# Large products of a hybrid encoder layer as plain fp32 matmuls, with the weights loaded straight into a ring of four tiles

## The reference

```python
proj = rms_norm(h, mix_norm) @ w_in                      # 1024 x 2048
att  = mla_group(proj[..., :352], ...)                   # 8 heads of latent attention, chunk-causal
rw   = rwkv7_group(token_shift(proj[..., 352:], mu), ...)  # 8 heads of a linear recurrence
h = h + concatenate([att, rw]) @ w_out                   # 1024 x 1024
q = rms_norm(h, ca_norm) @ wq; k, v = rms_norm(mem, mem_norm) @ wkv   # 256 memory tokens
h = h + softmax(q k^T / 16) v @ wo                       # 4 heads of 256
h = h + square(relu(rms_norm(h, mlp_norm) @ w_up)) @ w_down   # 4096 hidden features
out = rms_norm(h, final_norm)
```

## Time and profile before

| what | value |
|---|---|
| time, median of 3 runs | 2378.82 us (2354.41 to 2385.33) |
| span of the profiled execution | 2361.8 us, first to last instruction |
| TensorE busy in it | 2097.7 us, 89% |
| VectorE, ScalarE, GpSimd busy | 854.9, 410.0, 477.2 us |
| mean granted TensorE clock | 0.900 of full speed |

### The profile page before, as it was taken

One profiled execution on the slowest core, in us unless ns is written; L12 is line 12 of the kernel. 1 busy time (PEld: TensorE's weight loads), 2 busy tenths in 40 slices (PEclk: granted clock), 3 DMA queues, 4 the chain that ended last, 5 costly groups with the idle time before them and its releaser, 6 DMA issues.

```text
span 2361.8 us, 28991 instructions
## 1 busy us (share of the span) xinstructions
PE 2097.7 (89%) x10464; PEld 1634.2 (69%) x10464; DVE 854.9 (36%) x1424; ACT 410.0 (17%) x762; POOL 477.2 (20%) x280
## 2 busy tenths in 40 slices
PE   5999779887988898889498798797999999999996
PEld 4887358546755664666388785586888888888885
DVE  5223463345345433643633503425311211211333
ACT  3001311221122122211311302202100100100210
POOL 2321010001001000100120130121433333333431
PEclk9997779857987796779699999898999999999998
DMA  3110120002000200010312210010111111111111
GB/s 133 53 44 13 45 61 2 9 1 61 2 10 7 54 1 10 21 41 1 125 39 85 89 53 1 18 44 27 46 52 44 53 44 53 44 51 47 44 53 71
DMA packets 74499, 97.86 MB, mean 41 GB/s; under 512 B 28720, under 2 KB 54832, under 8 KB 74160
## 3 DMA queue, kind: packets, MB, share of 16 engines
q1 hardware_dynamic: 74416, 96.76, 12.2%
HBM read 85.19 MB, written 11.55 MB: 41 GB/s over the span
## 4 chain that ended last, share of the span: by engine, by line
PE 74%; DVE 12%; issue 9%; ACT 2%; DMA 1%; POOL 1%; DVEq 0%; SPq 0%; ACTq 0%; POOLq 0%
PE PS L563 47%; PE PS L684 3%; PE PS L661 2%; PE PS L1046 1%; PE PS L675 1%; DVE tmp L1378 1%; PE PS L983 1%; PE PS L641 1%; PE PS L706 1%; PE PS L643 1%; PE PS L711 1%; PE PS L664 1%; PE PS L837 1%; PE PS L822 1%; PE PS L647 1%
## 5 line engine op out<-in xcount | busy, mean ns | idle before, releaser
L563 PE MATMUL PS<-xn,wsp 128*128 128x512 f32 x3456 | 795.8, 392 | 16.2 <-DVE xn L1371 13.0
L563 PEld LDWEIGHTS PS<-xn,wsp 128*128 128x128 f32 x3456 | 653.7, 189 | 157.3 <-issue 11.5
L563 PE MATMUL PS<-hid,wsp 128*128 128x512 f32 x1536 | 348.8, 389 | 0.0
L563 PEld LDWEIGHTS PS<-hid,wsp 128*128 128x128 f32 x1536 | 288.4, 188 | 59.8
L479 POOL CAST wsp<-wraw 128x1024 fp32r<-128x1024 f32 x104 | 110.5, 1062 | 918.5 <-PE PS L563 767.9
L481 POOL TENSOR_TENSOR wsp<-wraw,wsp 128x1024 fp32r<-128x1024 f32 x104 | 283.2, 2723 | 8.3
L1341 ACT ACTIVATE tmp<-PS 128x1024 f32<-128x1024 f32 x32 | 32.9, 1028 | 494.2 <-PE PS L563 494.2
L1859 DVE TENSOR_TENSOR tmp<-tmp 128x1024 f32<-128x1024 f32 x32 | 39.2, 1225 | 211.7 <-ACT tmp L1341 211.7
L1874 DVE TENSOR_TENSOR H<-PS,H 128x1024 f32 x24 | 29.4, 1225 | 218.6 <-PE PS L563 218.6
L661 PE MATMUL PS<-H 128*128 128x512 f32 (+2 forms) x192 | 101.8, 649 | 0.8 <-DVE H L1519 0.6
L684 PE MATMUL PS<-sa,H 128*128 x576 | 89.6, 312 | 4.8 <-DVE H L1533 4.8
(11 more groups left out here) (269 smaller groups left out, 2564.1 us busy)
## 6 DMA issues: line engine op xcount, KB each, us to landing
wraw<-in_weights_dram SPq DMA_DIRECT2D x120, 512.0 KB, 3.2
H<-in_x_dram SPq DMA_DIRECT2D x16, 512.0 KB, 7.3
H<-x_dram SPq DMA_DIRECT2D x32, 128.0 KB, 2.5
H<-xt_dram SPq DMA_DIRECT2D x32, 128.0 KB, 2.7
out_dram<-proj SPq DMA_DIRECT2D x8, 512.0 KB, 3.0
a_dram<-sc_w SPq DMA_DIRECT2D x12, 256.0 KB, 2.3
sc_s<-in_head_weights_dram SPq DMA_DIRECT2D x4, 320.0 KB, 3.0
x_dram<-sa SPq DMA_DIRECT2D x1, 1032.0 KB, 4.0
```

Of the source, the lines that this page charges most:

```text
L563: last = nc.tensor.matmul(PS[:, 2 * k + half, :], wsp[:, k, kt, a, :], src[:, kt, b, HALF * half:HALF * half + HALF], start=(kt == 0 and ( ...
```

## The change

The three passes become one plain fp32 matmul for each half, so the heads and rests go everywhere: the weights', the inputs', the memory tokens', the cross attention output's and the hidden tiles'. Weights go from DRAM into a ring of four tiles (`RING` = 4), and TensorE reads them there. SyncE refills a place of the ring when TensorE has finished the unit that was in it. The normed inputs are scaled directly into `xn`; the output product reads `mixed`. The memory values are made with the tokens as the stationary operand, so that they come out turned, in two products of 128 columns for each input tile. ScalarE's relu frees the accumulators. The reload of `x` no longer waits for rests. Places in memory are laid out anew. The core of the diff:

```diff
+        xn = sa[:, 0:8192].rearrange("p (k t) -> p k t", k=KT)
+        hid = proj[:, 0:KT, :]
+        ring = sc_s[:, :].rearrange("p (b k n) -> p b k n", b=RING, k=KT)
...
+        def done(u):
+            return u + RING + 1
+        def freed(u):
+            return u + 3
...
-                with sp.Fori(0, n // 2) as i:
-                    for k in range(2):
-                        if U_MK + 2 <= u0 <= U_Q + 1:
-                            sp.wait_ge(mem_split, 2 * i + (u0 - U_MK - 1 + k))
-                        else:
-                            sp.wait_ge(w_split, 2 * i + (by_pool(u0) + k + 1))
-                        sp.dma_start(wraw[:, k, :], wall[bass.ds(2 * i + (u0 + k), 1)].rearrange(
-                            "a p n -> (a p) n")).then_inc(raw_loaded[k], 16)
+                with sp.Fori(0, n // RING) as i:
+                    for b in range(RING):
+                        sp.wait_ge(acc_ready, RING * i + done(u0 + b - RING))
+                        sp.dma_start(ring[:, b], wall[bass.ds(RING * i + (u0 + b), 1)].rearrange(
+                            "a p (k n) -> (a p) k n", k=KT)).then_inc(w_loaded[b], 16)
...
-            weights(U_OUT, 2)
+            weights(U_OUT, RING)
             for kt in range(KT):
-                sp.wait_ge(xn_ready, KT + kt + 1)
                 sp.dma_start(H[:, kt, :], x_t[kt]).then_inc(x_loaded[kt], 16)
...
+            def unit(u, turn, b, src, ready):
+                k = b % 2
+                pe.wait_ge(w_loaded[b], 16 * (turn + 1))
                 pe.wait_ge(acc_free, u + 1)
                 for kt in range(KT):
                     ready(kt)
-                    for a, b in ((0, 0), (0, 1), (1, 0)):
-                        for half in range(2):
-                            last = nc.tensor.matmul(
-                                PS[:, 2 * k + half, :], wsp[:, k, kt, a, :],
-                                src[:, kt, b, HALF * half:HALF * half + HALF],
-                                start=(kt == 0 and (a, b) == (0, 0)), stop=(kt == KT - 1 and a == 1))
+                    for half in range(2):
+                        last = nc.tensor.matmul(PS[:, 2 * k + half, :], ring[:, b, kt, :],
+                                                src(kt)[:, HALF * half:HALF * half + HALF],
+                                                start=(kt == 0), stop=(kt == KT - 1))
...
+                    for t in range(2):
+                        for kt in range(KT):
+                            last = nc.tensor.matmul(PS[:, 2 * (b % 2), win(t)], memn[:, kt, win(t)], ring[:, b, kt, :],
+                                                    start=(kt == 0), stop=(kt == KT - 1))
...
-            def scale_and_split(n, pas, gain, between=lambda kt: None):
...
+            def scale(n, gain):
                 dve.wait_ge(nb_ready, n + 1)
                 for kt in range(KT):
+                    nc.vector.scalar_tensor_tensor(xn[:, kt, :], H[:, kt, :], vec[:, gain + kt:gain + kt + 1],
+                                                   two(5), ALU.mult, ALU.mult).then_inc(xn_ready, 1)
...
-                        nc.scalar.activation(tmp[:, k, :], two(2 * k), ACT.Relu).then_inc(relu_ready, 1)
-                        act.wait_ge(hsq_ready, n + (k + 1))
-                        nc.scalar.copy(hid[:, bass.ds(2 * i + k, 1), 0, :].rearrange("p a t -> p (a t)"),
-                                       tmp[:, k, :]).then_inc(hhead_ready, 1)
+                        nc.scalar.activation(tmp[:, k, :], two(2 * k), ACT.Relu).then_inc(acc_free, 1)
```

More of the change, by code:

```diff
@@ L549, in gemm @@
             def gemm(u0, n, src, ready):
[L551 to L557 removed]
+                with pe.Fori(0, n // RING) as i:
+                    for b in range(RING):
+                        unit(RING * i + (u0 + b), i + u0 // RING, b, src, ready)
+            def unit(u, turn, b, src, ready):
+                k = b % 2
+                pe.wait_ge(w_loaded[b], 16 * (turn + 1))
                 pe.wait_ge(acc_free, u + 1)
@@ L973, in _, with mixed_ready @@
             last.then_inc(mm_pe, 1)
-            gemm(U_OUT, 8, xn, split_ready(1))
-            with pe.Fori(0, 4) as i:
-                for k in range(2):
-                    pe.wait_ge(mem_split, 2 * i + (k + 1))
-                    pe.wait_ge(acc_free, 2 * i + (U_MK + k + 1))
-                    pe.wait_ge(mm_dve, 10 + 2 * KT)
+            def mixed_ready(kt):
+                if kt == 0:
+                    pe.wait_ge(R_DVE.sem, R_DVE.at("out", PAIRS - 1))
+                    pe.wait_ge(MO_DVE.sem, MO_DVE.at("out", PAIRS - 1))
@@ L981, in _ @@
+            gemm(U_OUT, 8, mixed, mixed_ready)
+            pe.wait_ge(mm_dve, 10 + KT)
+            with pe.Fori(0, 2) as i:
+                for b in range(RING):
+                    pe.wait_ge(w_loaded[b], 16 * (i + (U_MK // RING + 1)))
+                    pe.wait_ge(acc_free, RING * i + (U_MK + b + 1))
                     for kt in range(KT):
-                        for a, b in ((0, 0), (0, 1), (1, 0)):
-                            last = nc.tensor.matmul(PS[:, 2 * k, 0:MEM], wsp[:, k, kt, a, :], memn[:, kt, b, :],
-                                                    start=(kt == 0 and (a, b) == (0, 0)), stop=(kt == KT - 1 and a == 1))
+                        last = nc.tensor.matmul(PS[:, 2 * (b % 2), 0:MEM], ring[:, b, kt, :], memn[:, kt, :],
+                                                start=(kt == 0), stop=(kt == KT - 1))
@@ L1004, in _ @@
-            turn_values(7)
-            gemm(U_Q, 8, xn, split_ready(2))
+            with pe.Fori(0, 2) as i:
+                for b in range(RING):
+                    pe.wait_ge(w_loaded[b], 16 * (i + (U_MV // RING + 1)))
+                    pe.wait_ge(acc_free, RING * i + (U_MV + b + 1))
+                    for t in range(2):
+                        for kt in range(KT):
+                            last = nc.tensor.matmul(PS[:, 2 * (b % 2), win(t)], memn[:, kt, win(t)], ring[:, b, kt, :],
+                                                    start=(kt == 0), stop=(kt == KT - 1))
+                    last.then_inc(acc_ready, 1)
@@ L1088, in norm @@
                 nc.scalar.activation(small[:, 8:16], small[:, 0:8], ACT.Sqrt).then_inc(std_ready, 1)
-            def heads(n):
-                for kt in range(KT):
-                    act.wait_ge(scaled, KT * n + kt + 1)
-                    nc.scalar.copy(xn[:, kt, 0, :], tmp[:, kt % 2, :]).then_inc(head_ready, 1)
             for kt in range(KT):
@@ L1247, in _ @@
                 nc.scalar.activation(mSt, mSt, ACT.Sqrt).then_inc(MO_ACT.sem, MO_ACT.one("std"))
-            for kt in range(KT):
-                act.wait_ge(R_DVE.sem, R_DVE.at("out", PAIRS - 1))
-                act.wait_ge(MO_DVE.sem, MO_DVE.at("out", PAIRS - 1))
-                nc.scalar.copy(xn[:, kt, 0, :], mixed(kt)).then_inc(head_ready, 1)
             act.wait_ge(mem_loaded, 16)
```

276 lines of the change are left out of this document (72 added, 204 removed).

## The result

The changed kernel takes 2633.11 us, median of 4 runs (2627.61 to 2638.35), against 2379.21 us for the kernel before (2354.41 to 2385.33, 4 runs). The ratio is 1.1081, with a 95% interval of 1.102 to 1.1143: slower by 254 us. The predicted time was 2641 us. The profiled execution of the changed kernel took 2630.86 us, with a span of 2627.9. In the experiments, executions more than 1.5% slower than the fastest of their kernel are left out of the medians and ratios.

What follows compares the result with a forecast made beforehand. TensorE streaming its passes, busy 89% of the span, was taken as the bound. Stage terms, chiefly projection +40.8, queries +22.8, second output product +23.0 and MLP +178.8, summed to 262; 2378.8 + 262 = 2641 us, range 2600 to 2690.

Steps and rivals of the forecast that it cites:

- The price of the plain pass: Large products: 0.430 us a pass, 13.76 us a unit against 10.9, some 298 us more over 104 units.
- The higher bound of 0.442: Large products: if long plain runs pay the reduced pass's excess of 0.012, a pass is 0.442, sum 40 us more.
- the third rival: Large products: plain fp32 costs four present passes, 14.5 us a unit, 78 us more, 2719 us; 6%.
- Projection: First large product, 16 units: first product at about 26.2, 4.1 us lost to low clock, end 250.5, later by 40.8.
- MLP: Last large products, 64 units: 706.8 us become 885.6, with 3.7 us for the low clock at the start; +178.8.
- Head groups: The 945 us after the projection: only tile names and semaphore counts edited, so 0.
- Before the output product: From the head groups' end: eight heads and rests go, memory chain sets the start, 1170.3 against 1178.39.
- Output product, keys, norm, values: After the head groups: 111.7, 27.6, 5.9 and 28.6 us plus 2.5 cold start; four stages end 2.1 us later.
- the fourth rival: Memory products: the weight ring starves, 2 us for each of 16 units, 32 us, 2673 us; 3%.
- Cross attention: The 96.4 us after the queries: VectorE's eight rests and a shared split go, -4.5, bounds 0 and -8.
- A cheaper pass in a long stream: Large products: neutral at 0.351 us a pass, about 2308 us at 0.33; 2%, plus 2% for within 2%.
- A falling clock under plain products: MLP: at clock 0.9 its 881 us grow by some 98, to 2739 us; 4%.

Runs made afterwards that it cites:

- the first experiment: Kernel before, all heads and rests still made, but one plain fp32 product replaces the three passes in the large products: 2671.95 us, ratio 1.1234.
- the pass orders: Kernel before with the 48 passes of a unit in another order in each large-product stage except the MLP: 2367.67 us.
- the last version: Kernel before with plain memory products, memory tokens loaded and squared earlier, and VectorE's two small norm steps ahead of its eight rests: 2355.53 us, ratio 0.9911.

## Why the prediction was right, step by step

**The price of the plain pass: right.** 0.430 was read from short runs; 3328 passes measured 0.4292. The higher bound of 0.442, by the excess of the reduced pass over half of 0.430, is refuted: half of the plain pass is 0.2146, shorter than the reduced one. The first experiment, with the product alone, measured +296 us for a term of 298.

**Four passes (the third rival): refuted as a price; as a count it fits, and isn't shown.** The rule of the Trainium skill ("FP8 and Floating Point Precision", section "TensorE Precision Notes"), four passes for true FP32, would give 0.907 at the present price of a pass, and four such passes measured 0.907. The plain pair measured 0.858. The Trainium skill ("TensorE: Matmul & The Clock Gate", section "Wait — 56ns, not 53.3ns?") puts matmuls from start to start at their columns over 2.4 GHz plus about 2.5 ns, which for 1024 columns is an estimate of 429.2 ns: this agrees with the plain pass at 429.17, if a recorded pass streams its 512 columns twice. By the same rule the reduced pass would take 215.8 ns, and the traces have 226.67: there the measurement decides.

**Projection (+40.8, measured +36.7) and MLP (+178.8, measured +173.8): passes right, the clock terms wrong.** I added 4.1 and 3.7 us for a product that starts at the low clock. In the changed kernel the clock is 1.00 from 24.90 on. The rows at half clock belong to kernels in which the product is fed in pieces: at the start of the MLP all eight traces with the splitting have them and the four without have none. At the start of the projection only four of the eight have them, so there the trace that I read held one of two cases. In that stage the kernel before loses nothing by it: its projection ends at 209.46 at the low clock, and at 209.46 with the clock at 1.00 from 29 to 34 (the run with plain memory products). (In the sum, 8 us at half speed are 4.0, not 4.1.) Scaling one tile takes 1.28 us and TensorE needs 1.72 for it, as worked out, so it has no pause; I had drawn that, and not that the low clock would go with it. Why it goes isn't shown.

**Head groups (0, measured +22.1): wrong in this trace, and the largest term of the error.** The code is unchanged, and so is the work of the other engines, but the time isn't. It goes with the granted clock, over 40 us, and the trace of before happened to be at the short end. For the same reason the first large product of the output stage starts at 1228.7 and not near 1211. I should have given this stage bounds of its own from the granted clock. What sets the clock's course in it stays open. Between the two profiled spans, 266 apart, these 22 us hide that the other stages came out 18 us below the forecast. The medians differ by 254 us against a predicted 262, and which part of that the head groups hold isn't known.

**Before the output product (-8.1, measured -8.3): right.** The seven additions and one copy took 3.5 us, for which I had taken 4, and the landing of the tokens and the start of the square came as worked out. The chain of the changed kernel from there on:

```profile
1214.84 5.67 DMA proj<-in_mem_dram
1228.94 112.14 PE PS L517 x256
1341.09 27.63 PE PS L946 x128
1371.13 2.05 PE PS L537 x16
1373.18 28.59 PE PS L956 x256
1401.77 109.88 PE PS L517 x256
```

**Output product, keys, norm, values (111.7, 27.6, 5.9, 28.6 + 2.5): right but for the norm and the cold start.** The chain has 112.1, 27.6 and 28.6. The norm takes 4.5 us, from 1368.72 to 1373.2, with its 16 matmuls in 2.05 us where the kernel before has 3.43, since the clock stays at 1.00, and the values start without the 2.5 us. These are 3.9 us. The clock isn't the change's in every execution: with a ring of two it falls there too. The ring never starved (the fourth rival); with two tiles it would have cost 4.

**Queries (+22.8, measured +22.5): right. Cross attention (-4.5, measured -8.1): at its better bound, mostly by the clock.** Its granted clock also rises, from 0.91 to 0.98, and the clock has more of the gain than the splitting. From the end of the queries to the next large product, the traces with the splitting left in take 96.6 us at clock 0.91 (the kernel before, four passes, the pass orders), 95.3 at 0.93 (the first experiment) and 91.7 at 0.98 (the run with plain memory products, and the last version); the changed kernel takes 88.5 at 0.98. The run with plain memory products, then the changed kernel:

```profile
1432.60:1524.30 91.70, 68.21 (x257) 43.36 (x257) 48.32 (x89) 28.02 (x75) 15.12 (x16) 0.98 0.04 12
1511.70:1600.00 88.30, 68.09 (x256) 43.25 (x256) 37.59 (x81) 27.99 (x75) 8.13 (x12) 0.98 0.02 6
```

At equal clock the removed rests and splits are worth some 3.2 us, less than my 4.5, and some 4.9 go with the clock, for which I had nothing. So my term was right in kind, a little too large, and its total fell short for another reason.

**Its output product (+23.0, measured +21.1): 1.9 too much**, the slow start that I carried over from the kernel before and that went with the splitting. It starts at 1600.10 at full clock. **Norm (-0.8, measured -1.3): right.**

**The rivals.** A cheaper pass in a long stream: 0.4292 in every large product at full clock, refuted. A falling clock under plain products: 1.00 through the MLP, refuted.

## What to carry to other kernels

Where TensorE is busy throughout, count passes times spacing, and read the spacing from start to start in the trace, at the width and type in question: a plain fp32 product of 512 columns is 0.858 us and three reduced passes are 0.680, and taking work from VectorE and GpSimd left that spacing as it was. Where TensorE waits for a splitting, as in the small memory products, the same plain product is the faster one, so choose stage by stage. And give a stage whose granted clock wanders bounds of its own, even if nobody edits it, since a profile shows one draw of it.

## What was not expected of the hardware

A reduced-type pass of 512 columns takes 226.67 ns in every order of passes, 12.1 ns more than half of the plain one (429.17 / 2 = 214.6), and 234.3 ns with a constant stationary tile, in three kernels; the cause of either is open. The head groups took from 945.7 to 986.3 us with the same instructions, TensorE's granted clock going from 0.805 to 0.764: 1.7% of the whole time. That is about as much as the runs of one kernel differ among themselves (36.5 us over 23 of the kernel before), but only profiled executions show where they differ.
